# Four of twelve convolution-input products per layer, computed from seven part products

## The reference

```
h = h + 0.5 * swiglu(rms_norm(h, ffn1_norm), ffn1_w_in, ffn1_w_out)
u = rms_norm(h, mix_norm)
(z_s, xbc, dt_s, qkv, z_d, b_d, a_d, gate_s, gate_d) = split(u @ w_in)
# mamba2 branch
xbc = silu(causal_depthwise_conv(xbc, conv_w, conv_b))     # width 4
xs, Bm, Cm = split(xbc)                # 2048, 512, 512 features
y_s = ssd_chunked(xs, dt, a, Bm, Cm) ...
# deltanet branch on qkv, then merge, w_out, and a second swiglu
```

## Time and profile before

| what | value |
|---|---|
| time, median of 3 runs | 3397.73 us (3390.92 to 3399.65) |
| profiled execution, its own time | 3394.11 us |
| its span, first to last instruction | 3392.0 us |
| mean granted TensorE clock | 0.993 |
| TensorE busy | 3321.7 us, 98% of the span |
| VectorE busy | 2019.5 us, 60% |
| ScalarE busy | 641.6 us, 19% |

### The profile page before, as it was taken

The page is one execution under the profiler, slowest core; times in us unless marked ns, Lnnn a source line. Parts: engine busy times, 40 slices in busy tenths (PEclk is TensorE's granted clock), DMA queues, the critical chain, the costliest instruction groups (busy, mean ns, idle before and its releaser), DMA issues.

```text
span 3392.0 us, 54681 instructions
## 1 busy us (share of the span) xinstructions
PE 3321.7 (98%) x23134; PEld 3080.8 (91%) x23134; DVE 2019.5 (60%) x4578; ACT 641.6 (19%) x1415; POOL 241.4 (7%) x320
## 2 busy tenths in 40 slices
PE   8999999999999999998999999999999999999998
PEld 8998888889999988888899999988899999878998
DVE  6655575237666445754166678762387688642585
ACT  1112232121111132321211101202211101211211
POOL 0200000100102000001002000020003000210031
PEclk9999999999999999999999999999999999999999
DMA  5443342234444433432354444344344444343443
GB/s 189 166 158 134 131 147 104 80 124 174 163 169 166 162 137 128 146 123 69 117 185 162 148 153 172 136 153 149 112 174 162 162 162 166 122 156 129 149 164 135
DMA packets 80772, 495.15 MB, mean 146 GB/s; under 512 B 16880, under 2 KB 20880, under 8 KB 21392
## 3 DMA queue, kind: packets, MB, share of 16 engines
q1 hardware_dynamic: 70896, 490.57, 40.9%
q10 hardware_dynamic: 9632, 1.08, 0.2%
HBM read 490.03 MB, written 1.59 MB: 145 GB/s over the span
## 4 chain that ended last, share of the span: by engine, by line
PE 90%; DVE 6%; ACT 1%; DMA 1%; issue 1%; ACTq 0%; SPq 0%; DVEq 0%
PE bank L331 83%; PE bank L1756 1%; PE bank L1819 1%; PE bank L1812 1%; PE bank L480 1%; DVE arena L883 1%; DVE arena L881 1%; DVE arena L885 0%; DVE arena L1329 0%; PE bank L2380 0%; PE bank L2441 0%; PE bank L1732 0%; PE bank L2424 0%; PE bank L1795 0%; DVE arena L880 0%
## 5 line engine op out<-in xcount | busy, mean ns | idle before, releaser
L331 PE MATMUL bank<-arena,ring 128*128 128x128 f32 (+1 forms) x6032 | 1043.4, 328 | 14.5 <-DMA ring<-w 11.4
L331 PEld LDWEIGHTS bank<-arena,ring 128*128 128x128 f32 x6032 | 931.1, 192 | 104.4 <-issue 27.9
L331 PE MATMUL bank<-xT,ring 128*128 128x128 f32 (+1 forms) x5952 | 1012.8, 327 | 0.0
L331 PEld LDWEIGHTS bank<-xT,ring 128*128 128x128 f32 x5952 | 907.0, 191 | 74.9 <-issue 0.7
L331 PE MATMUL bank<-arena 128*128 128x128 f32 x7008 | 830.0, 275 | 2.4 <-DVE arena L885 2.3
L331 PEld LDWEIGHTS bank<-arena 128*128 128x128 f32 x7008 | 805.7, 192 | 3.2 <-DVE arena L885 3.2
L880 DVE TENSOR_TENSOR arena<-ring 128x512 f32<-128x512 f32 x270 | 186.3, 690 | 121.0 <-PE bank L331 108.9
L837 ACT ACTIVATE arena<-bank 128x128 f32<-128x128 f32 x228 | 63.1, 277 | 956.0 <-PE bank L331 951.2
L912 DVE TENSOR_TENSOR arena<-arena,bank 128x256 f32<-128x256 f32 x228 | 95.3, 418 | 177.7 <-ACT arena L837 177.4
L331 PE MATMUL bank<-xT,arena 128*128 128x128 f32 x1504 | 199.1, 275 | 0.2
L1329 DVE SCALAR_TENSOR_TENSOR arena<-arena,par 128x256 f32<-128x256 f32 x288 | 118.0, 480 | 133.0 <-ACT arena L1046 128.5
(11 more groups left out here) (285 smaller groups left out, 2384.4 us busy)
## 6 DMA issues: line engine op xcount, KB each, us to landing
ring<-w SPq DMA_DIRECT2D x462, 1024.0 KB, 4.8
hT<-hT_d SPq DMA_DIRECT2D x4, 256.0 KB, 3.5
arena<-memT_d SPq DMA_DIRECT2D x1, 1024.0 KB, 7.4
outT<-hT SPq DMA_DIRECT2D x4, 256.0 KB, 2.2
cst<-cst_d SPq DMA_DIRECT2D x1, 796.5 KB, 10.8
arena<-dmask_d SPq DMA_DIRECT2D x1, 768.0 KB, 10.3
par<-p SPq DMA_DIRECT2D x2, 216.0 KB, 5.1
par<-p SPq DMA_DIRECT2D x1, 376.5 KB, 5.4
```

The costliest lines, as they stand in the source:

```text
L331: ins = self.e.matmul(out, lhsT, rhs, start=start, stop=stop)
```

## The change

Products 2, 5, 8 and 11 of xbc, in both layers of the first block, are computed from seven part products. Weight sums lie where z_d and gate_s will be, token sums where gate_d will be, and `join` writes straight into `pad`. ScalarE's tap for these products reads `pad` and not PSUM. VectorE makes the token sums right after the first product's copy. It makes the weight sums of product n + 1 ahead of `conv(n)`, in n = 1, 4, 7 and 10. The other eight products stay.

```diff
+THIRDS = (2, 5, 8, 11)
 def bulk_jobs():
...
-        spec += many(L, "xbc", 1, "dve") + many(L, "xbc", 11, "act", 1) + many(L, "z_s", 8, "dve") + many(L, "qkv", 12, "act") + both(L, "z_d", 4) + both(L, "gate_s", 4)
+        for i in range(12):
+            spec += [((L, "xbc_7", (i // 3, b)), "dve") for b in range(2)] if i in THIRDS else many(L, "xbc", 1, "act" if i else "dve", i)
+        spec += many(L, "z_s", 8, "dve") + many(L, "qkv", 12, "act") + both(L, "z_d", 4) + both(L, "gate_s", 4)
...
+        self.seven_xbc = Seven(arena, 40 * S + 24 * S, 40 * S + 40 * S, sums_at + 4096)
+        self.seven_xbc.c = self.pad[:, :, :, 3:3 + S]
...
     def conv_in(n):
...
-        if n == 0:
+        if n == 0 or name == "xbc" and i in THIRDS:
-            e.wait_ge(sems.bulk_read_dve, BULK.read(L, name, i))
-            for t in range(2):
-                ins = e.activation(dst[:, t, :], m.pad[:, 0, t, 3:3 + S], ACT.Identity, scale=col("xbc_w", 4 * t + 3),
+            if n:
+                part_by_act(a, m.seven_xbc, L, "xbc_7", n // 3)
+                e.wait_ge(sems.bulk_read_dve, BULK.read(L, "xbc_7", (n // 3, 1)))
+            else:
+                e.wait_ge(sems.bulk_read_dve, BULK.read(L, name, i))
+            for kk in range(2):
+                t = 2 * n + kk
+                ins = e.activation(dst[:, t, :], m.pad[:, n % 2, kk, 3:3 + S], ACT.Identity, scale=col("xbc_w", 4 * t + 3),
                                    bias=col("xbc_b", t))
...
     pair_opened_by_dve(v, m, L, "xbc", m.pad[:, 0, :, 3:3 + S])
+    tokens_by_dve(v, m, m.seven_xbc, 3 * L + 1, TOKENS_FROM[L, "xbc_7"])
...
     for n in range(12):
+        if n + 1 in THIRDS:
+            weights_by_dve(v, m.seven_xbc, ring, FAST_FROM[L, "xbc_7"] + n // 3)
+        if n in THIRDS:
+            join(v, m.seven_xbc, L, "xbc_7", n // 3, in_place=True)
+            if ROWS_AT <= n < ROWS_AT + 8:
+                rows(n - ROWS_AT)
         conv(n)
-        if ROWS_AT <= n < ROWS_AT + 8:
+        if ROWS_AT <= n < ROWS_AT + 8 and n not in THIRDS:
             rows(n - ROWS_AT)
...
     for i in range(1, 12):
-        if i > 1:
+        if i in THIRDS:
+            t.by_seven(L, "xbc_7", (i // 3,), m.seven_xbc, 3 * L + 1, opens=False)
+        elif i > 1:
             t.product((L, "xbc", i), xT)
```

More of the change, by code:

```diff
@@ L235, in clear @@
         self.nc.all_engine_barrier()
-PER1 = {"silu_ready": 2 * KF, "conv_done": 24, "features_ready": 12, "qkv_tanh": 12, "qkv_ready": 12, "z_tanh": 8, "gates_ready": 8, "base_solved": 1, "zd_gated": 4,
+PER1 = {"opened": 5, "silu_ready": 2 * KF, "conv_done": 24, "features_ready": 12, "qkv_tanh": 12, "qkv_ready": 12, "z_tanh": 8, "gates_ready": 8, "base_solved": 1, "zd_gated": 4,
         "y_summed": 4, "small_by_dve": 4, "small_by_act": 5, "dt_ready": 1, "split_ready": 1,
@@ L419, in opening, with by_seven @@
                 ins.then_inc(sems.bulk_done, 1)
-    def by_seven(self, L, name, n, sums, norm=None, by_token=False):
+    def by_seven(self, L, name, n, sums, norm=None, by_token=False, opens=True):
         e, sems = self.e, self.sems
@@ L431, in ready @@
                 e.wait_ge(sems.tx_by_dve, TOKENS_FROM[L, name] + made[what])
-        for i in range(n):
+        for i in range(n) if isinstance(n, int) else n:
             X, Y = self.open_bulk(L, name, (i, 0)), self.open_bulk(L, name, (i, 1))
-            if norm is not None and i == 0:
+            if opens and norm is not None and i == 0:
                 self.opening((X[:, 0:S], Y[:, 0:S]), (True, True), norm)
                 continue
-            new = norm is not None and i == 1
+            new = norm is not None and i == opens
             self.seven(sums, FAST_FROM[L, name] + i, range(GROUPS), X, Y, lambda what, g: where[what](g), True, True,
@@ L599, in multiply_fast @@
     FAST_FROM[L, name] = len(FAST) - opening
-    FAST.extend(range(at + opening, at + chunks))
+    FAST.extend(range(at + opening, at + chunks) if isinstance(chunks, int) else [at + i for i in chunks])
     PARTS_FROM[L, name], state[0] = state[0] - opening, state[0] + parts - opening
@@ L608 @@
     multiply_fast(_L, "down1", _L * CHUNKS1 + KF, KF // 2, PAIRS, False)
+    multiply_fast(_L, "xbc_7", _L * CHUNKS1 + 33, THIRDS, 4, True)
     multiply_fast(_L, "z_d", _L * CHUNKS1 + 65, 4, 4, True)
@@ L1023, in conv_in @@
         dst = m.xbc if name == "xbc" else m.qkv
-        if n == 0:
-            e.wait_ge(sems.bulk_read_dve, BULK.read(L, name, i))
-            for t in range(2):
-                ins = e.activation(dst[:, t, :], m.pad[:, 0, t, 3:3 + S], ACT.Identity, scale=col("xbc_w", 4 * t + 3),
+        if n == 0 or name == "xbc" and i in THIRDS:
[7 more added lines that the diff above has]
+                ins = e.activation(dst[:, t, :], m.pad[:, n % 2, kk, 3:3 + S], ACT.Identity, scale=col("xbc_w", 4 * t + 3),
                                    bias=col("xbc_b", t))
             ins.then_inc(sems.opened, 1)
+            seen.up("opened")
             return
@@ L1316, in conv @@
         dst, w = (m.xbc, "xbc_w") if name == "xbc" else (m.qkv, "qkv_w")
-        if n:
+        if n == 0 or name == "xbc" and i in THIRDS:
+            e.wait_ge(sems.opened, upto(L, "opened", (n + 1) // 3 + 1))
+        else:
             e.wait_ge(sems.bulk_read_act, BULK.read(L, name, i))
-        else:
-            e.wait_ge(sems.opened, L + 1)
         for tap in range(3):
```

## The result

The changed kernel takes 3408.03 us (median of 8 runs, 3405.27 to 3410.79), the kernel before 3397.28 us in its 8 runs (3390.92 to 3399.66). The ratio is 1.0031, 95% interval 1.0022 to 1.0041. It is slower, as forecast, but by 10.8 us and not by 18.9, and it lies 1 us under the stated range. The profiled execution took 3406.79 us with a span of 3404.9 us.

What follows compares the result with a forecast made beforehand. TensorE, busy for 98% of the span, was taken to bound the kernel. Two stalls (19.3 us) plus slow restarts (4.8) less the saving (5.2) gave +18.9 us, 3416.6 us against the 3397.7 median; range 3409 to 3424.

Steps and rivals of the forecast that it cites:

- Direction: Whole kernel: slower, at 0.90, with about the same at 0.08 and faster at 0.02.
- saving: TensorE, eight xbc products over two layers: each falls from 6.91 to 6.26 us, 5.2 us less in all.
- stall: TensorE in product 2 waits 9.66 us for VectorE's weight sums, which stand behind conv(0); two layers, 19.3 us.
- restart: TensorE after each product 2 stall: lowered clock loses 2.4 us, 4.8 us in all.
- later sums: Weight sums of products 5, 8, 11: VectorE has them 2.1 us before TensorE asks; cost 0.
- token sums: Four VectorE operations, some 2.7 us, in its 8.59 us idle before the small product; cost 0.
- joins: VectorE's five operations per seven-part product, 1.46 us; conv starts some 0.5 us later; cost 0.
- 2.0 us of room: After product 11, the last silu ends 2.0 us before TensorE comes; 0.5 to 1.0 of that goes, cost 0.
- the sum: Whole kernel: stalls 19.3 plus restarts 4.8 less saving 5.2 gives +18.9 us, 3416.6 us against the median.
- rival 3: TensorE's later waits (base_d DMA, VectorE at L1486) absorb the stall, leaving 5.2 us of gain, 3392.5 us; chance 0.05.
- the rival that the clock does not fall after the stall: TensorE after product 2's stalls: no clock loss that matters, +14.1 us, 3411.8 us; chance 0.09.
- The range: Whole kernel: 3409 to 3424 us, taking in the clock rival below and late VectorE at later sums above.

Runs made afterwards that it cites:

- e1: Changed kernel with the weight sums of product 2 made earlier, right behind the token sums; 3387.81 us, ratio 0.9973 to the kernel before.
- before_3: The kernel before, unchanged, run a third time for another trace; 3397.83 us.
- e2: Kernel before, with TensorE held in product 2 after 4 of 16 matmuls until product 1's convolution is done, each layer; 3417.33 us, ratio 1.0056.
- nodma_after: Changed kernel without the first block's DMA round trip of diagonal blocks and its waits, block inverses left out; 3390.49 us.
- nodma_before: Kernel before without the first block's DMA round trip of diagonal blocks and its waits, block inverses left out; 3375.11 us.
- warm_before: Kernel before without the DMA round trips (block inverses left out), with thrown-away constant matmuls filling TensorE's waits at the norms; 3366.82 us.

## Why the prediction was wrong, point by point

- **Direction, saving, stall, restart: right.** The stall was 9.4 us twice (9.66 forecast), the clock cost 2.3 and 2.6 us (2.4), a product from seven 6.25 us (6.26), each stage +9.2 and +9.5 us (9.4). e1 showed that moving only the late sums takes the loss away. The direction holds for that reason, and not by luck.
- **The later sums, the token sums and joins: right.** No wait at products 5, 8 and 11. At the end of the stage the last silu ends at 332.12 and TensorE comes at 333.52, so 1.4 us of the 2.0 us of room are left.
- **The step that failed is the sum.** It added the stages' 18.9 us to a kernel behind them that was taken as unchanged: what the shift does to TensorE's later restarts and round trips was put at nothing. The prediction gave "TensorE's later idle times shrink" only as rival 3, with 0.05 and with the wrong mechanism (a chain that does not start on TensorE), and of the later waits it left out the four of 2.0 us on ScalarE. The stages were 18.4 us longer in the mean of two traces. Without the round trips 15.4 us of it arrived at the end, and with the restarts at the norms filled as well all of it, 18.5. So 3 us are restarts that fell more kindly once every later instant had moved, and the other 4.6 us (15.4 - 10.8) go with the presence of the round trips. Each of these steps is uncertain by some 2 to 3 us.
- **The traces give the same account.** In before_3 the four stretches of the table are 50.0 50.1, 38.3 39.3, 35.4 34.9 and 82.2 82.2 us. Both layers together, the mean of two traces after lies under the mean of three before by 1.4, 2.4, 0.9 and 2.5 us, 7.2 in all: 18.4 - 7.2 = 11.2, against 10.8 measured. For e1 the same sum gives -9.0 (measured -10.0), for e2 +20.4 (19.6). The 2.4 us are the store of base_d, which ran without a weight load beside it in L1 of both traces after and in no layer before. That a shift of 9 to 19 us would put it there could not be read from the rows of the kernel before, and no run tested it alone.
- **The range** had 3409 as its lower end, by the rival that the clock does not fall after the stall. It should have carried a term for all that stands behind the stage: the four stretches vary by 1.5 to 3.8 us each between the traces of these two kernels.

## What to carry to other kernels

Ask of each new operand when the engine that makes it gets there in its own order, and not how busy that engine is: here VectorE was idle before, and the same four operations cost 12 us a layer in one place and nothing 15 us earlier. Where TensorE stops and restarts many times, a local change of some 20 us moves each later restart and each transfer against the weight stream, and several us come or go that way: 7 to 8 of 18 here. Judge such a change by its stage in the trace as well as by the time. Fill or close the gaps before comparing small variants, and see whether a short transfer on the chain shares the DMA engines with a weight load in one variant and not in the other.

## What the runs showed of the hardware

The same wait of 1.96 us left the clock at 2.4 GHz in nodma_after and was followed by 1.2 GHz in nodma_before (16 records in 3.62 and 4.68 us, granted clock 1.00 and 0.73 over 4 us). It also differs between traces of one kernel: from o to the sum of squares the three traces before have 80.5 to 83.9 us. The clock was also at half for a while without any wait, right behind the small product of 48 columns (0.68 over 4 us in warm_before).

Nine and four matmuls on constants, thrown away, in waits of 4.1 and 2.0 us made the kernel before faster by 12.5 us (ratio 0.9963) and by 8.3 us without the round trips, though they compute nothing that is used. Of the 4 us between these two gains, 2.9 stand at the round trip and behind it in the trace of the filled kernel before.

A store of 128 KB took 1.7 us where no weight load landed beside it, and 2.9 to 5.3 us where 0.27 to 1.05 MB of weights did.
